# Half-size GpSimd subtractions in a Hymba decoder layer

## The chip, the cores and the metric

The kernel runs on one core of a Trainium2 chip. The metric is the device time of one execution in microseconds; less is better.

## The reference

One decoder layer over 512 tokens of width 1024, in float32. Cut to the parts that matter here:

```python
x = x + 0.5 * swiglu(rms_norm(x, ffn1_norm), ffn1_w_gate, ffn1_w_up, ffn1_w_down)   # D_FF = 2816
z = rms_norm(x, mix_norm) @ w_in            # 1024 -> 1280: pool group | q | k | v
merged = [rms_norm(causal_pool_mixer(u)), rms_norm(sliding_window_sink_attention(q, k, v))]
x = x + merged @ w_out
x = x + 0.5 * swiglu(rms_norm(x, ffn2_norm), ffn2_w_gate, ffn2_w_up, ffn2_w_down)
gate = sigmoid(rms_norm(x, ple_norm) @ w_ple_gate)
x = x + gate * (p @ w_ple_proj)
```

`swiglu(h, g, u, d)` is `(silu(h @ g) * (h @ u)) @ d`. All products are wanted at float32 precision.

## The kernel before, in words

Every product is made of three matmuls in the rounded type float32r: a matrix is split into a rounded part (hi) and the rest (lo), and hi x hi, lo x hi and hi x lo are summed in PSUM (`product`, L1584 to L1588). The kernel is written engine by engine, with counting semaphores between the engines; the order on each engine is the order in which the code stands.

**The weights.** They come in chunks of 128 partitions by 1024 columns, by DMAs on SyncE's queue, into a ring of four slots `raw`. ScalarE rounds a chunk into `w_hi` (`split`, L530). GpSimd subtracts: `w_lo = raw - w_hi` (`lo_of`, L403 to L406), and raises `w_ready`. TensorE waits for `w_ready` before it uses the chunk and raises `w_used` after it; SyncE waits for `w_ready` before it loads the slot again. GpSimd so makes 85 chunks' rests at L405. Its list mixes them with a few sums of the mixing stage (`win_sum`, `pool_sum`, `y_sum`).

**The gate and up projections of each FFN.** There are 22 column blocks f of 128. Four are plain. For the other 18, TensorE forms the two products with seven half-size products in place of eight, from sums of weight halves (Strassen's scheme in Winograd's form), in a loop over pairs of blocks. For each block VectorE makes the weight sums `sa` and `sb_f` (1024 columns each, `sums`, L1071 to L1078), ScalarE rounds them (L607, L616) and half of a gate chunk (L603), and GpSimd makes the rests in `fast_lo`: L415 (512 columns, the half gate chunk), L418 (1024, `sa`), L422 (1024, `sb_f`). The rest of the up chunk is made by VectorE itself (`u_rest`, L1083, 1024 columns). L422 waits for it:

```python
pool.wait_ge(sa_hi, m + 1)
pool.tensor_tensor(lo_at(sa_slot(c0, p)), sa[:], f32(hi_at(sa_slot(c0, p))),
                   ALU.subtract).then_inc(w_ready, 1)
pool.wait_ge(w_hi_done, f * 2 + c0 + 2)
pool.wait_ge(u_ready, m + 1)
```

On TensorE a block of the loop is seven parts of 12 matmuls (`pair`, L1654 to L1678). The first waits for `u_ready` (L1083), the second and third for `w_ready` (L418, L422), the last for `c_made`, the adds on VectorE at L1094, of which one stands behind L1083.

**The down projection of each FFN.** It runs in two halves of the output columns, 11 chunks each. The left operand is split anew for each chunk: ScalarE rounds (L631), VectorE makes the rest (`act_rest`, L1117, 1024 columns, both operands in SBUF). When the first half is complete, VectorE updates the residual: per block of 128 rows L1192 (PSUM times `rstd`) and L1194 (`x_t` plus `tmp`, both in SBUF, 512 columns). ScalarE then rounds the new `x_t` (L539) and squares it (L551), VectorE makes its rests (`h_rest`, L1022) and in the first FFN adds the squares (L1031). The roundings for the next chunks of the second half stand behind these in ScalarE's list, L1117 behind them in VectorE's.

**Other names.** In the fast loop's start VectorE makes sums of the left operand (L1126 to L1134) and their rests (L1059). L1431 is a rest of a sum in the mixing stage.

Of the kernel before, what the change touches and what calls it, by code (L numbers as in the profile page):

```python
# [7 lines left out]
ALU = mybir.AluOpType  # L8
# [10 lines left out]
def layer(nc, x, p, ffn1_norm, ffn1_w_gate, ffn1_w_up, ffn1_w_down, mix_norm, w_in, pool_w, pool_scale,  # L19
# [36 lines left out]
    WH = CHUNK // 2  # L56
# [11 lines left out]
    with es:  # L68
        def sb(name, shape, dt=F32, stack=es):
            return stack.enter_context(nc.sbuf_tensor(name, shape, dt))  # L70

        def sem(name):
            return es.enter_context(nc.semaphore(name))
# [17 lines left out]
        raw = sb("raw", [P, SLOTS, CHUNK])  # L91
        w_hi = sb("w_hi", [P, SLOTS, CHUNK], F32R)
        w_lo = sb("w_lo", [P, SLOTS, CHUNK], F32R)
# [7 lines left out]
        with ExitStack() as phase:  # L101
# [5 lines left out]
            sa = sb("sa", [P, CHUNK], stack=phase)  # L107
# [34 lines left out]
        sb_f = tmp[:, 2:4, :].rearrange("p a c -> p (a c)")  # L142
# [11 lines left out]
        def w_at(tile, extra, slot):  # L154
            return tile[:, slot, :] if slot < SLOTS else extra[:, slot - SLOTS, :]

        def hi_at(slot):
            return w_at(w_hi, wx_hi, slot)

        def lo_at(slot):  # L160
            return w_at(w_lo, wx_lo, slot)
# [4 lines left out]
        def sa_slot(c0, p):  # L166
            return (c0 + 2) % SLOTS if p else SLOTS

        def sb_slot(c0, p):
            return (c0 + 3) % SLOTS if p else SLOTS + 1  # L170

        def g_cols(p):
            return slice(p * WH, (p + 1) * WH)

        def raw_g(c0, p):
            return (c0 + 2 * p) % SLOTS
# [12 lines left out]
        w_hi_done, w_ready, w_used = sem("w_hi_done"), sem("w_ready"), sem("w_used")  # L189
# [51 lines left out]
        def f32(ap):  # L241

            return ap.bitcast(F32)
# [153 lines left out]
        def _(pool):  # L397
# [4 lines left out]

            def lo_of(slot, count):  # L403
                pool.wait_ge(w_hi_done, count)
                pool.tensor_tensor(w_lo[:, slot, :], raw[:, slot, :], f32(w_hi[:, slot, :]),  # L405
                                   ALU.subtract).then_inc(w_ready, 1)  # L406

            def fast_lo(n, c0):

                with pool.Fori(2, QUADS) as quad:  # L410
                    for p in range(2):
                        f = quad * 2 + p
                        m = f + n * FAST - PLAIN
                        pool.wait_ge(g_hi, m + 1)
                        pool.tensor_tensor(wx_lo[:, 2, g_cols(p)], raw[:, raw_g(c0, p), WH:],  # L415
                                           f32(wx_hi[:, 2, g_cols(p)]), ALU.subtract)
                        pool.wait_ge(sa_hi, m + 1)
                        pool.tensor_tensor(lo_at(sa_slot(c0, p)), sa[:], f32(hi_at(sa_slot(c0, p))),  # L418
                                           ALU.subtract).then_inc(w_ready, 1)
                        pool.wait_ge(w_hi_done, f * 2 + c0 + 2)  # L420
                        pool.wait_ge(u_ready, m + 1)
                        pool.tensor_tensor(lo_at(sb_slot(c0, p)), sb_f, f32(hi_at(sb_slot(c0, p))),  # L422
                                           ALU.subtract).then_inc(w_ready, 1)

            for slot in range(SLOTS):
                lo_of(slot, FFN1 + SLOTS + slot + 1)
            fast_lo(0, FFN1)
            with pool.Fori((FFN1 + GU) // SLOTS, (C_K + 2) // SLOTS) as quad:
                for slot in range(SLOTS):
                    lo_of(slot, quad * SLOTS + slot + 1)  # L430
# [40 lines left out]
            def y_sum(b):  # L471
# [6 lines left out]
                    .then_inc(y_summed, 1)  # L478

            lo_of(0, C_Q + 2)  # L480
            lo_of(1, C_Q + 3)
            lo_of(2, C_Q3 + 1)
# [26 lines left out]
            for c in range(C_WA + HALF - 1, FFN2 + 2 * SLOTS):  # L509
                lo_of(c % SLOTS, c + 1)  # L510
            fast_lo(1, FFN2)
            down = -(-(FFN2 + GU) // SLOTS)
            for c in range(FFN2 + GU, down * SLOTS):
# [1605 lines left out]
```

## Time and profile before

| what | value |
|---|---|
| time, median of 3 runs | 914.07 us (912.55 to 914.72) |
| the profiled execution's own time | 912.49 us |
| its span in the profile | 910.7 us |
| TensorE busy, matmuls | 893.5 us (98%) |
| VectorE / ScalarE / GpSimd busy | 541.8 / 496.5 / 475.3 us |
| GpSimd at L405 | 85 x 2587 ns = 219.2 us |
| GpSimd at L418 | 36, 96.3 us |
| GpSimd at L422 | 36 x 2402 ns = 86.4 us |
| GpSimd at L415 (512 columns) | 36 x 1312 ns = 47.2 us |

The span is what the profiler sees of the execution; 1.8 us of the execution's time lie outside it. Engines: PE is TensorE, DVE VectorE, ACT ScalarE, POOL GpSimd, SP SyncE. Busy time counts an operation from its start to its end in the record, so time in which an operation has started and waits inside the engine counts as busy.

### The profile page before, as it was taken

Reading aid. Unit: us, or ns where it says so; the run is one execution under the profiler, and the core shown is the slowest. Engines: PE = TensorE matmul, PEld = TensorE weight load, DVE = VectorE, ACT = ScalarE, POOL = GpSimd, SP = SyncE. Lnnn points to the kernel's source line nnn. Section 1 sums busy time; section 2 is a strip of 40 time slices with the busy share of each in tenths; the row PEclk is TensorE's granted clock in tenths of the full one; section 3 lists DMA queues with packets and bytes.
Section 4 is the critical chain, followed back from the end, with each engine's and each line's share of the span. In section 5 each row is a group of like instructions: output and inputs, shape, how many; then the busy total and the mean of one; then the engine's idle time right before and its main releaser. Section 6 shows DMA issues by size and latency. Waiting matters only on the chain.

```text
span 910.7 us, 15441 instructions
## 1 busy us (share of the span) xinstructions
PE 893.5 (98%) x5462; PEld 798.7 (88%) x5462; DVE 541.8 (59%) x819; ACT 496.5 (55%) x777; POOL 475.3 (52%) x228
## 2 busy tenths in 40 slices
PE   9989999999999999999999999999999999989998
PEld 7779999999988778887788879999999988878887
DVE  7586766676422733778958586667666522652552
ACT  5765666566433633668834756556655533433451
POOL 0446666666554364266665346666665564355430
PEclk9999999999999999999999999999999999999999
DMA  7523333333333244221324233333333253223311
GB/s 200 160 59 115 115 92 98 110 115 92 109 122 92 70 115 102 60 81 48 70 70 120 65 93 93 101 106 114 92 106 103 90 162 93 91 92 93 94 69 46
DMA packets 131049, 89.33 MB, mean 98 GB/s; under 512 B 11552, under 2 KB 116296, under 8 KB 131016
## 3 DMA queue, kind: packets, MB, share of 16 engines
q1 hardware_dynamic: 131000, 88.90, 32.9%
q8 instruction: 19, 0.31, 0.1%
q14 instruction: 14, 0.11, 0.0%
q10 hardware_dynamic: 16, 0.00, 0.0%
HBM read 86.80 MB, written 2.10 MB: 98 GB/s over the span
## 4 chain that ended last, share of the span: by engine, by line
PE 86%; DVE 7%; ACT 4%; issue 2%; DMA 0%; SPq 0%; DVEq 0%; ACTq 0%
PE bank L1586 28%; PE bank L1587 28%; PE bank L1588 28%; PE bank L1601 1%; DVE wx_lo L1117 1%; ACT act_f L579 1%; DVE x_t L1194 1%; ACT w_hi L530 1%; DVE tmp L1192 1%; PE bank L1857 1%; DVE w_lo L1083 1%; DVE act_f L1129 0%; ACT tmp L575 0%; DMA raw<-in_ffn_w_up 0%; DVE h_lo L1022 0%
## 5 line engine op out<-in xcount | busy, mean ns | idle before, releaser
L405 POOL TENSOR_TENSOR w_lo<-raw,w_hi 128x1024 fp32r<-128x1024 f32 x85 | 219.2, 2587 | 246.1 <-ACT w_hi L530 246.1
L1586 PE MATMUL bank<-h_hi,w_hi 128*128 128x256 f32 (+1 forms) x700 | 228.2, 326 | 3.9 <-DVE w_lo L1083 3.9
L1588 PE MATMUL bank<-h_hi,w_lo 128*128 128x256 f32 (+1 forms) x700 | 226.8, 324 | 0.0
L1587 PE MATMUL bank<-h_lo,w_hi 128*128 128x256 f32 (+1 forms) x700 | 226.8, 324 | 0.0
L1117 DVE TENSOR_TENSOR wx_lo<-act_f,wx_hi 128x1024 fp32r<-128x1024 f32 x44 | 65.7, 1497 | 145.7 <-ACT wx_hi L631 145.6
L1586 PEld LDWEIGHTS bank<-h_hi,w_hi 128*128 128x128 f32 x700 | 133.2, 190 | 16.0 <-DVE w_lo L1083 4.8
L1588 PEld LDWEIGHTS bank<-h_hi,w_lo 128*128 128x128 f32 x700 | 133.3, 190 | 10.7
L1586 PE MATMUL bank<-wx_hi,w_hi 128*128 128x512 f32 x352 | 137.9, 392 | 4.9 <-DVE wx_lo L1117 4.9
L1587 PEld LDWEIGHTS bank<-h_lo,w_hi 128*128 128x128 f32 x700 | 133.3, 190 | 10.0
L1587 PE MATMUL bank<-wx_lo,w_hi 128*128 128x512 f32 x352 | 137.7, 391 | 0.0
L1588 PE MATMUL bank<-wx_hi,w_lo 128*128 128x512 f32 x352 | 137.5, 391 | 0.0
L631 ACT ACTIVATE wx_hi<-act_f 128x1024 fp32r (+1 forms) x44 | 46.6, 1059 | 130.6 <-PE bank L1588 130.5
L530 ACT ACTIVATE w_hi<-raw 128x1024 fp32r<-128x1024 f32 x85 | 88.6, 1049 | 35.6 <-PE bank L1588 35.6
L415 POOL TENSOR_TENSOR wx_lo<-raw,wx_hi 128x512 fp32r<-128x512 f32 x36 | 47.2, 1312 | 94.9 <-ACT wx_hi L603 94.9
L1586 PEld LDWEIGHTS bank<-wx_hi,w_hi 128*128 128x128 f32 x352 | 66.5, 189 | 19.5 <-DVE wx_lo L1117 5.7
L1586 PE MATMUL bank<-xs_hi,wx_hi 128*128 128x256 f32 x288 | 82.3, 286 | 0.3 <-ACT sumsq L622 0.3
L1587 PE MATMUL bank<-xs_lo,wx_hi 128*128 128x256 f32 x288 | 82.1, 285 | 0.0
L1588 PE MATMUL bank<-xs_hi,wx_lo 128*128 128x256 f32 x288 | 82.0, 285 | 0.0
L1094 DVE TENSOR_TENSOR tmp<-bank,sumsq 128x256 f32<-128x256 f32 x72 | 30.6, 425 | 81.6 <-PE bank L1588 81.6
L1588 PEld LDWEIGHTS bank<-wx_hi,w_lo 128*128 128x128 f32 x352 | 66.5, 189 | 14.0
L1587 PEld LDWEIGHTS bank<-wx_lo,w_hi 128*128 128x128 f32 x352 | 66.4, 189 | 13.5
L575 ACT ACTIVATE tmp<-tmp 128x512 f32<-128x512 f32 x44 | 27.7, 630 | 91.6 <-DVE tmp L1100 85.1
(232 smaller groups left out, 1891.0 us busy)
## 6 DMA issues: line engine op xcount, KB each, us to landing
raw<-in_ffn_w_down SPq DMA_DIRECT2D x44, 512.0 KB, 3.7
raw<-in_ffn_w_gate SPq DMA_DIRECT2D x42, 512.0 KB, 3.8
raw<-in_ffn_w_up SPq DMA_DIRECT2D x42, 512.0 KB, 3.8
raw<-in_w_ple_gate SPq DMA_DIRECT2D x8, 512.0 KB, 3.7
raw<-in_w_in SPq DMA_DIRECT2D x6, 512.0 KB, 3.9
raw<-in_w_in SPq DMA_DIRECT2D x8, 256.0 KB, 3.5
raw<-in_w_out SPq DMA_DIRECT2D x4, 512.0 KB, 3.4
raw<-in_w_out SPq DMA_DIRECT2D x8, 256.0 KB, 4.1
```

The lines of the kernel that those rows point to most:

```text
L405: pool.tensor_tensor(w_lo[:, slot, :], raw[:, slot, :], f32(w_hi[:, slot, :]), ALU.subtract).then_inc(w_ready, 1)
L415: pool.tensor_tensor(wx_lo[:, 2, g_cols(p)], raw[:, raw_g(c0, p), WH:], f32(wx_hi[:, 2, g_cols(p)]), ALU.subtract)
L530: nc.scalar.activation(w_hi[:, slot, :], raw[:, slot, :], ACT.Copy).then_inc(w_hi_done, 1)
L575: nc.scalar.activation(a, a, ACT.Silu).then_inc(silu_done, 1)
L579: nc.scalar.activation(hf[d // HALF][:, d % HALF, :], x_t[:, d, :], ACT.Copy, scale=gain[:, 2 * n * KD + d:2 * n * KD + d + 1]).then_inc(h ...
L631: nc.scalar.activation(wx_hi[:, par, :].rearrange("p (a c) -> p a c", a=2), act_f[:, bass.ds((g - half) * 2, 2), :], ACT.Copy).then_inc(ac ...
L1083: nc.vector.tensor_tensor(lo_at(u_slot(c0, p)), raw[:, raw_u(c0, p), :], f32(hi_at(u_slot(c0, p))), ALU.subtract).then_inc(u_ready, 1)
L1094: nc.vector.tensor_tensor(dst, src[:, 0:TH], old, ALU.add).then_inc(c_made, 1)
L1117: nc.vector.tensor_tensor(wx_lo[:, par, :].rearrange("p (a c) -> p a c", a=2), act_f[:, bass.ds((g - half) * 2, 2), :], f32(wx_hi[:, par, ...
L1586: nc.tensor.matmul(dst, a_hi, b_hi, start=first, stop=False, skip_group_check=more)
L1587: nc.tensor.matmul(dst, a_hi, b_lo, start=False, stop=False, skip_group_check=more)
L1588: return nc.tensor.matmul(dst, a_lo, b_hi, start=False, stop=last, skip_group_check=more)
```

## The change

Each GpSimd subtraction of 1024 columns (`lo_of`, and the two of `fast_lo`) is written as two of 512 columns, one behind the other. The semaphore wait stands ahead of the first, the semaphore is raised by the second. `WH` is 512. Nothing else is changed.

```diff
             def lo_of(slot, count):
                 pool.wait_ge(w_hi_done, count)
-                pool.tensor_tensor(w_lo[:, slot, :], raw[:, slot, :], f32(w_hi[:, slot, :]),
+                pool.tensor_tensor(w_lo[:, slot, 0:WH], raw[:, slot, 0:WH], f32(w_hi[:, slot, 0:WH]), ALU.subtract)
+                pool.tensor_tensor(w_lo[:, slot, WH:], raw[:, slot, WH:], f32(w_hi[:, slot, WH:]),
                                    ALU.subtract).then_inc(w_ready, 1)
...
                         pool.wait_ge(sa_hi, m + 1)
-                        pool.tensor_tensor(lo_at(sa_slot(c0, p)), sa[:], f32(hi_at(sa_slot(c0, p))),
-                                           ALU.subtract).then_inc(w_ready, 1)
+                        lo, hi = lo_at(sa_slot(c0, p)), f32(hi_at(sa_slot(c0, p)))
+                        pool.tensor_tensor(lo[:, 0:WH], sa[:, 0:WH], hi[:, 0:WH], ALU.subtract)
+                        pool.tensor_tensor(lo[:, WH:], sa[:, WH:], hi[:, WH:], ALU.subtract).then_inc(w_ready, 1)
                         pool.wait_ge(w_hi_done, f * 2 + c0 + 2)
                         pool.wait_ge(u_ready, m + 1)
-                        pool.tensor_tensor(lo_at(sb_slot(c0, p)), sb_f, f32(hi_at(sb_slot(c0, p))),
-                                           ALU.subtract).then_inc(w_ready, 1)
+                        lo, hi = lo_at(sb_slot(c0, p)), f32(hi_at(sb_slot(c0, p)))
+                        pool.tensor_tensor(lo[:, 0:WH], sb_f[:, 0:WH], hi[:, 0:WH], ALU.subtract)
+                        pool.tensor_tensor(lo[:, WH:], sb_f[:, WH:], hi[:, WH:], ALU.subtract).then_inc(w_ready, 1)
```

The instructions of GpSimd before, from the chunks ahead of the fast loop (L405) to the first block of the loop's body, with the semaphores that they wait for:

```order
L405 TENSOR_TENSOR w_lo<-raw,w_hi 128x1024 [waits w_hi_done] x4
L410 UNCONDITIONAL_BRANCH
L410 ISA
L415 TENSOR_TENSOR wx_lo<-raw,wx_hi 128x512 [waits g_hi]
L418 TENSOR_TENSOR wx_lo<-sa,wx_hi 128x1024 [waits sa_hi]
L420 ISA
L422 TENSOR_TENSOR wx_lo<-tmp,wx_hi 128x1024 [waits u_ready,w_hi_done]
```

And the same stretch now, from the last of these chunks on:

```order
L405 TENSOR_TENSOR w_lo<-raw,w_hi 128x512 [waits w_hi_done]
L406 TENSOR_TENSOR w_lo<-raw,w_hi 128x512
L411 UNCONDITIONAL_BRANCH
L411 ISA
L416 TENSOR_TENSOR wx_lo<-raw,wx_hi 128x512 [waits g_hi]
L420 TENSOR_TENSOR wx_lo<-sa,wx_hi 128x512 [waits sa_hi]
L421 TENSOR_TENSOR wx_lo<-sa,wx_hi 128x512
L422 ISA
L425 TENSOR_TENSOR wx_lo<-tmp,wx_hi 128x512 [waits u_ready,w_hi_done]
L426 TENSOR_TENSOR wx_lo<-tmp,wx_hi 128x512
```

No instruction changes its place; each subtraction of 1024 columns is two rows, of which the second waits for no semaphore. The lists of the other engines are the same but for line numbers.

## Rows read from the trace of the kernel before

**Rows 1.** The page: busy time, share of the span and instructions by engine

```profile
PE 893.5 (98%) x5462; PEld 798.7 (88%) x5462; DVE 541.8 (59%) x819; ACT 496.5 (55%) x777; POOL 475.3 (52%) x228
```

**Rows 2.** Timeline, TensorE: start, us, operation, [idle before, who ended it]

```profile
57.75 0.39 PE L1586 MATMUL bank<-h_hi,w_hi 128*128 128x256 f32 x1 [2.96 <-DVE w_lo L1083]
68.42 0.39 PE L1586 MATMUL bank<-h_hi,wx_hi 128*128 128x256 f32 x1 [0.24 <-DVE tmp L1094]
...
319.95 0.50 PE L1586 MATMUL bank<-wx_hi,w_hi 128*128 128x512 f32 x1 [2.29 <-DVE wx_lo L1117]
...
540.45 0.39 PE L1586 MATMUL bank<-h_hi,w_hi 128*128 128x256 f32 x1 [0.96 <-DVE w_lo L1083]
...
802.96 0.64 PE L1586 MATMUL bank<-wx_hi,w_hi 128*128 128x512 f32 x1 [2.61 <-DVE wx_lo L1117]
```

**Rows 3.** Windows: stretch, us, busy (count) of PE, PEld, DVE, ACT, POOL, clock, DMA

```profile
803.00:807.00 4.00, 4.00 (x11) 3.17 (x12) 3.22 (x1) 0.00 (x0) 2.14 (x1) 0.57 0.50 154
320.00:324.00 4.00, 4.00 (x18) 3.27 (x19) 3.23 (x1) 0.00 (x0) 4.00 (x2) 1.00 0.57 166
```

**Rows 4.** Timeline, GpSimd and VectorE, start of the first fast loop

```profile
54.24 2.37 POOL L418 TENSOR_TENSOR wx_lo<-sa,wx_hi 128x1024 fp32r<-128x1024 f32 x1 [0.77 <-ACT wx_hi L607]
...
55.14 2.56 DVE L1083 TENSOR_TENSOR w_lo<-raw,w_hi 128x1024 fp32r<-128x1024 f32 x1 [0.75 <-ACT w_hi L612]
```

**Rows 5.** Timeline, VectorE and TensorE, inside the first fast loop

```profile
116.68 1.43 DVE L1083 TENSOR_TENSOR w_lo<-raw,w_hi 128x1024 fp32r<-128x1024 f32 x1
118.03 0.41 DVE L1094 TENSOR_TENSOR tmp<-bank,tmp 128x256 f32<-128x256 f32 x1
...
118.92 0.28 PE L1586 MATMUL bank<-h_hi,w_hi 128*128 128x256 f32 x1
```

**Rows 6.** Timeline, GpSimd and VectorE, residual update of the first FFN

```profile
303.47 2.48 POOL L405 TENSOR_TENSOR w_lo<-raw,w_hi 128x1024 fp32r<-128x1024 f32 x1 [2.96 <-ACT w_hi L530]
...
304.34 2.17 DVE L1194 TENSOR_TENSOR x_t<-x_t,tmp 128x512 f32<-128x512 f32 x1
306.55 0.69 DVE L1192 SCALAR_TENSOR_TENSOR tmp<-bank,rstd 128x512 f32<-128x512 f32 x1
307.27 0.69 DVE L1194 TENSOR_TENSOR x_t<-x_t,tmp 128x512 f32<-128x512 f32 x1
```

**Rows 7.** Timeline, GpSimd and VectorE, ahead of the gap at 319.95

```profile
315.80 3.02 POOL L405 TENSOR_TENSOR w_lo<-raw,w_hi 128x1024 fp32r<-128x1024 f32 x1 [9.85 <-ACT w_hi L530]
...
316.84 3.05 DVE L1117 TENSOR_TENSOR wx_lo<-act_f,wx_hi 128x1024 fp32r<-128x1024 f32 x1 [0.27 <-ACT wx_hi L631]
...
318.78 3.37 POOL L405 TENSOR_TENSOR w_lo<-raw,w_hi 128x1024 fp32r<-128x1024 f32 x1
```

**Rows 8.** Lines L405 and L415: duration ns min/median/max, first and last start

```profile
L405 POOL TENSOR_TENSOR w_lo<-raw,w_hi x85: 2391/2608/3387, 29.1 to 886.7; 128x1024 fp32r<-128x1024 f32 x85
...
L415 POOL TENSOR_TENSOR wx_lo<-raw,wx_hi x36: 1293/1300/1543, 52.2 to 706.5; 128x512 fp32r<-128x512 f32 x36
```

**Rows 9.** Timeline, ScalarE, VectorE and GpSimd, mixing stage

```profile
440.06 1.12 ACT L530 ACTIVATE w_hi<-raw 128x1024 fp32r<-128x1024 f32 x1
...
443.57 0.94 DVE L1431 TENSOR_TENSOR d_lo<-sumsq,d_hi 128x512 fp32r<-128x512 f32 x1
...
443.90 2.87 POOL L405 TENSOR_TENSOR w_lo<-raw,w_hi 128x1024 fp32r<-128x1024 f32 x1
```

**Rows 10.** Timeline, VectorE, second block of the second fast loop

```profile
548.67 2.05 DVE L1083 TENSOR_TENSOR w_lo<-raw,w_hi 128x1024 fp32r<-128x1024 f32 x1 [0.96 <-ACT w_hi L612]
```

**Rows 11.** Timeline, VectorE, ahead of the first fast loop

```profile
41.95 2.33 DVE L1129 TENSOR_TENSOR act_f<-act_f 128x1024 f32<-128x1024 f32 x1
```

**Rows 12.** Timeline, VectorE and GpSimd, ahead of the gap at 802.96

```profile
796.70 2.90 DVE L1022 SCALAR_TENSOR_TENSOR h_lo<-x_t,gain,h_hi 128x512 fp32r<-128x512 f32 x1
...
799.01 2.81 POOL L405 TENSOR_TENSOR w_lo<-raw,w_hi 128x1024 fp32r<-128x1024 f32 x1
...
799.52 3.38 DVE L1117 TENSOR_TENSOR wx_lo<-act_f,wx_hi 128x1024 fp32r<-128x1024 f32 x1
```

## The prediction

> **What bounds the kernel now.** I read the page first: TensorE is busy for 98% of the span [rows 1], so what can be won or lost lies in its few gaps or in a clock that falls. Then the timeline of TensorE, for its gaps. The reader is to see the five on which the sum rests: 2.96 us at 57.75 and 0.24 at 68.42 in the first FFN, 0.96 at 540.45 in the second, and 2.29 at 319.95 and 2.61 at 802.96, where each FFN's down projection passes from its first half of the output columns to its second [rows 2]. GpSimd ends none of them; VectorE does. The windows after two of them come next: after the gap of 2.61 us the granted clock averages 0.57 over 4 us (so most of it is at the lower level, 1.2 GHz), after the gap of 2.29 it stays at 1.00, 2.4 GHz [rows 3]. At 0.57, 4 us do the work of 2.28: 1.72 us lost.
>
> Then the timelines of VectorE and GpSimd beside each other, at the operations that end these gaps. GpSimd's subtract of 1024 columns runs from 54.24 to 56.61; VectorE's L1083, 1024 columns with both operands in SBUF, starts at 55.14 and ends at 57.70, 1.09 us after GpSimd [rows 4]. In the loop it takes 1.43 us [rows 5]. So it stood still until GpSimd was done and then ran. An operation of 512 columns does the same: L1194 starts at 304.34 behind a subtract that ends at 305.95 and ends at 306.51, 0.56 later; its unhindered neighbour L1194 takes 0.69 [rows 6]. L1192, which has one operand in PSUM, takes 0.69 as well [rows 6]. Call this a hold. GpSimd is held likewise: the subtract that starts at 318.78 ends at 322.15, 2.26 us after the L1117 that ended at 319.89 [rows 7].
>
> **What the change does to each operation.** 85 subtracts at L405 and 72 in the fast loop (36 at L418, 36 at L422) become 314 of 512 columns. The whole one takes 2.39 us at least; the 512-column form is there already, at L415, with 1.29 at least and 1.54 at most [rows 8]. One subtract starts some 0.04 us before the row of the one ahead ends (318.78 against 315.80 + 3.02 [rows 7]). So a pair takes 1.29 + 1.29 - 0.04 = 2.54, 0.14 more than a whole one of 2.40; bounds: 0 (no fixed part is added) and 2 x 1.54 - 2.40 = 0.68. I take 0.14, since an unhindered L415 is at its minimum. That is 157 x 0.14 = 22 us more of GpSimd time, on an engine that is 52% busy [rows 1], and off TensorE's path unless one result is late.
>
> The other side is the hold: it should end after 1.29 us, not 2.39, if the waiting VectorE operation gets its turn between the halves. What happens then, [rows 9] show. The subtract at 443.90 had its input from 441.18 on, since the last rounding at L530 ran from 440.06 to 441.18. VectorE's L1431 asked at 443.57, while the subtract before was running, and yet it went first: it ended at 444.51, and the subtract took 2.87 instead of 2.40. A waiting VectorE operation thus goes ahead of GpSimd's next one, even one that has long been ready. Held GpSimd work of 512 columns should end 2.26 - 1.10 = 1.16 after the VectorE operation that held it.
>
> **Term by term.**
> *Starts of the fast loop, 57.75 and 540.45.* The first half ends at 54.24 + 1.29 = 55.53, L1083 at 56.62, 1.08 us earlier. What follows on the way to the loop's steady state passes another L1083, 2.05 us long [rows 10], which asks so late that it meets the second half: 0.14 back. I allow 0.25 for L1059 in the same chain, which can now meet the halves of L422. Gain 0.7 each, 1.4 in all; bounds 0.3 and 1.08 each. The lower clock after 57.75 is not counted: the gap at 68.42 is ended by VectorE again, so that chain, not the matmuls, set the time there. L1129 before it, held for 2.33 us [rows 11], gives nothing: L1131 stands right behind it, has two SBUF operands too, and will meet the second half.
>
> *Down projection, 319.95.* L1194 ends at 303.47 + 1.29 + 0.56 = 305.32, 1.19 earlier. The second half starts then and ends at 306.48. The next L1194 would start at 306.08 and ends at 306.48 + 0.56 = 307.04 instead of 307.96: 0.92 stays of 1.19. From there VectorE and ScalarE pass this on to the subtract at 315.80 and L1117 at 316.84 [rows 7]. L1117 waits for all of a subtract that ended at 318.82; with halves it waits 1.10 less. Sum 0.92 + 1.10 = 2.02, less than the gap's 2.29. Gain 2.0; bounds 1.1 and 2.29.
>
> *Down projection, 802.96.* The same 0.92 at its L1194. Then L1022 at 796.70 took 2.90, held by a subtract, 1.10 less with halves. Then L1117 asked at 799.52 and ended at 802.90, behind the whole subtract that started at 799.01 [rows 12]. L1022 now ends at 799.60 - 0.92 - 1.10 = 797.58, the waiting half at 798.74, L1117 at 799.83: 3.07 earlier, more than the gap of 2.61, so TensorE goes through. With the gap goes the fall of the clock: 1.72. Gain 4.3; bounds 1.1 (half the gap, clock still falls) and 4.3.
>
> *Fast loop.* L1083 at 116.68 falls into the second half, which ends 0.14 later. The combining add behind it at 118.03 ends at 118.44, and the part of the matmuls that needs it starts at 118.92 [rows 5]: cover 0.48, of which 0.14 is used. Nothing.
>
> *Everything else* (w_lo in the mixing stage and at the end, loads that wait for it on SP's queue) is hidden behind TensorE: no gap over 0.2 us, there or anywhere, is ended by GpSimd. If a w_lo came late, TensorE would wait at its chunk.
>
> **The sum.** 1.4 + 2.0 + 4.3 = 7.7 us. The profiled execution took 912.49 (span 910.7), which gives 904.8; it lay 1.6 below the median of 914.07, from which I forecast 906.4.
>
> **Rivals.**
> *The halves keep the port between them.* They have no wait of their own between them, while the subtract of [rows 9] had one, though fulfilled. Then each hold lasts 0.14 longer: one each at the two loop starts, two at 319.95, three at 802.96, so 7 x 0.14 = 1.0 us slower, 915.1, within 0.2%. The Trainium skill has a rule for this, in "SBUF — State Buffer", section "Who interferes with whom": GpSimd and a VectorE operation with two SBUF inputs share a port pair, which the one that issues first keeps for its whole instruction. Whether the second half counts as issued behind its first, ahead of the VectorE operation, it does not tell; if it does, this rival is the rule's result. That a hold lasts as long as the instruction, [rows 4] show (1.09 us after its end). Against the rival: [rows 9]. Chance 0.13.
>
> *The gain is lost behind another wait.* L1117 is earlier, but ScalarE's roundings or a load ends the two gaps, and the clock still falls: some 1 us gained, 913, within 0.2%. For it: each gap is the end of a chain of some twenty operations. Against: the timeline shows VectorE as what ended each. Chance 0.05.
>
> *The loop becomes bound by GpSimd: slower.* If a half costs 1.54, the longest L415, a pair adds 0.68. In the loop that is over the cover of 0.48 by 0.20, in 36 rounds 7.2 us; and without a turn between the halves the seven holds grow by 0.68 each, 4.8. Together +12, 926. It decides from 0.48 us per pair, and even with turns from 0.70 it outweighs all gains (36 x 0.22 = 7.9). For it: L415 did take 1.54 once. Against: its median is 1.30 [rows 8]. Chance 0.05.
>
> **How the numbers follow.** Forecast 0.77, the rivals 0.13, 0.05 and 0.05. A measurement of this kernel can tell about 0.2%, 1.8 us, from no change. Forecast's own bounds: gains of 1.08 x 2 + 2.29 + 4.3 = 8.8 and 0.6 + 1.1 + 1.1 = 2.8, so 905.3 to 911.3; with 1.3 below for the spread of the runs, 904.0 to 911.3. That holds nearly all of 0.77, and with the edges of the second rival some 0.8. Faster by over 0.2%: 0.77. Within: 0.13 + 0.05 = 0.18. Slower: 0.05.
>
> **What would show it.** Right: 314 subtracts of 1.3 us in place of 157; L1083 near 55.1 takes some 1.5; L1117 before the second half of the down projection some 2.0 after 316; the gap at 802.96 gone and no window there below a clock of 0.9; L1083 in the loop at 1.57, without gaps of TensorE. Wrong: L1083 at 2.7 (no turn between halves), a gap per round of the loop, or a half that takes over 1.5.

## The result and the profile after

The changed kernel takes **905.0 us** (median of 4, 904.89 to 905.4), the kernel before 913.56 in the same comparison (912.55 to 914.72): ratio 0.9907, 95% interval 0.989 to 0.9924. Forecast were 906.4 in 904.0 to 911.3. The profiled execution took 905.06 with a span of 903.2, beside 912.49 and 910.7 before. Line numbers after L407 are higher by 3 in the changed kernel (L1083 is L1086, L1117 is L1120, L1194 is L1197).

The page's busy times, which answer to [rows 1]:

```profile
PE 891.0 (99%) x5462; PEld 796.6 (88%) x5462; DVE 530.4 (59%) x819; ACT 496.7 (55%) x777; POOL 509.0 (56%) x385
```

GpSimd has 157 instructions more and is busy 33.7 us longer; VectorE, with the same instructions, is busy 11.4 less.

TensorE's timeline after, all its gaps between 50 and 70 us, then the one at the start of the second fast loop (start, us, operation, [idle before, who ended it]):

```profile
56.87 0.39 PE L1589 MATMUL bank<-h_hi,w_hi 128*128 128x256 f32 x1 [1.88 <-DVE w_lo L1086]
60.62 0.38 PE L1589 MATMUL bank<-xs_hi,wx_hi 128*128 128x256 f32 x1 [0.62 <-POOL wx_lo L426]
64.43 0.38 PE L1589 MATMUL bank<-h_hi,wx_hi 128*128 128x256 f32 x1 [0.69 <-ACT sumsq L625]
67.94 0.39 PE L1589 MATMUL bank<-h_hi,wx_hi 128*128 128x256 f32 x1 [0.39 <-DVE tmp L1097]
...
540.83 0.38 PE L1589 MATMUL bank<-xs_hi,wx_hi 128*128 128x256 f32 x1 [0.62 <-POOL wx_lo L426]
```

The gap of 2.96 of [rows 2] is 1.88, 1.08 less. Two of 0.6 to 0.7 stand behind it that were not there, one of them ended by GpSimd, which ended none over 0.2 us before. By the gaps alone nothing was gained here: they sum to 3.20 us before and to 3.58 after. But before, TensorE ran the matmuls behind the first gap partly at 1.2 GHz (the windows stand with e1), and after at 2.4. What counts is when VectorE's chain lets the matmuls at 68.42 (67.94 after) start, and that is 0.48 us earlier, or 0.67 with the 0.19 by which this execution was late before the loop.

VectorE and GpSimd at the start of the first fast loop:

```profile
54.44 1.30 POOL L420 TENSOR_TENSOR wx_lo<-sa,wx_hi 128x512 fp32r<-128x512 f32 x1 [0.77 <-ACT wx_hi L610]
55.69 2.27 POOL L421 TENSOR_TENSOR wx_lo<-sa,wx_hi 128x512 fp32r<-128x512 f32 x1
...
55.33 1.48 DVE L1086 TENSOR_TENSOR w_lo<-raw,w_hi 128x1024 fp32r<-128x1024 f32 x1 [0.75 <-ACT w_hi L615]
```

L1086 asks while the first half runs and ends 1.07 us after that half. The second half ends 1.15 us after L1086. So VectorE gets its turn between the halves. Beside [rows 4], 2.56 became 1.48.

The same two engines at the residual update and the second half of the first FFN's down projection, which answer to [rows 6, 7], with TensorE's gap:

```profile
302.99 1.38 POOL L405 TENSOR_TENSOR w_lo<-raw,w_hi 128x512 fp32r<-128x512 f32 x1 [2.81 <-ACT w_hi L533]
304.33 1.75 POOL L406 TENSOR_TENSOR w_lo<-raw,w_hi 128x512 fp32r<-128x512 f32 x1
...
303.86 1.07 DVE L1197 TENSOR_TENSOR x_t<-x_t,tmp 128x512 f32<-128x512 f32 x1
...
305.69 0.95 DVE L1197 TENSOR_TENSOR x_t<-x_t,tmp 128x512 f32<-128x512 f32 x1
...
315.52 1.98 DVE L1120 TENSOR_TENSOR wx_lo<-act_f,wx_hi 128x1024 fp32r<-128x1024 f32 x1 [0.26 <-ACT wx_hi L634]
...
317.55 0.50 PE L1589 MATMUL bank<-wx_hi,w_hi 128*128 128x512 f32 x1 [0.36 <-DVE wx_lo L1120]
```

L1197 takes 1.07 where L1194 took 2.17, and L1120 1.98 where L1117 took 3.05. The gap of 2.29 is 0.36.

The window that answers to the first of [rows 3] (us, busy time and count of PE, PEld, DVE, ACT, POOL, granted clock, DMA share, GB/s); the same matmuls start 5.7 us earlier now, at 797.3. Then VectorE ahead of it, for [rows 12]:

```profile
797.30:801.30 4.00, 4.00 (x19) 3.33 (x18) 1.65 (x1) 2.01 (x2) 3.70 (x3) 1.00 0.51 171
```

```profile
794.63 2.31 DVE L1120 TENSOR_TENSOR wx_lo<-act_f,wx_hi 128x1024 fp32r<-128x1024 f32 x1
798.79 1.65 DVE L1120 TENSOR_TENSOR wx_lo<-act_f,wx_hi 128x1024 fp32r<-128x1024 f32 x1 [1.85 <-ACT wx_hi L634]
```

There is no gap, and the granted clock is 1.00 (2.4 GHz) where its mean was 0.57.

Where the 7.45 us between the two profiles went, from the starts of the same matmuls in both, read at the last matmul of each place (minus is earlier):

| place | forecast | measured |
|---|---|---|
| the kernel's first 50 us | 0 | +0.19 |
| start of the first fast loop | -0.7 | -0.67 |
| down projection, 319.95 | -2.0 | -1.92 |
| mixing stage | 0 | +0.15 |
| start of the second fast loop | -0.7 | -0.68 |
| down projection, 802.96 | -4.3 | -4.52 |

### The profile page after: what moved, and what is told of

Read it like the earlier page. It is cut to its first block, busy times and chain, and to the rows that moved or that the text cites. A ratio compares the mean times of both kernels' runs of the same rounds, so it can differ in the third digit from the quotient of the medians.

```text
span 903.2 us, 15598 instructions
## 1 busy us (share of the span) xinstructions
PE 891.0 (99%) x5462; PEld 796.6 (88%) x5462; DVE 530.4 (59%) x819; ACT 496.7 (55%) x777; POOL 509.0 (56%) x385
## 4 chain that ended last, share of the span: by engine, by line
PE 88%; DVE 5%; ACT 4%; issue 2%; POOL 1%; DMA 0%; SPq 0%; DVEq 0%; POOLq 0%; ACTq 0%
PE bank L1589 29%; PE bank L1590 28%; PE bank L1591 28%; PE bank L1604 1%; ACT act_f L582 1%; ACT w_hi L533 1%; PE bank L1860 1%; DVE act_f L1134 0%; DVE wx_lo L1120 0%; DMA raw<-in_ffn_w_up 0%; ACT tmp L578 0%; DVE x_t L1197 0%; DVE sumsq L1034 0%; DVE tmp L1195 0%; POOL wx_lo L425 0%
## 5 line engine op out<-in xcount | busy, mean ns | idle before, releaser
L405 POOL TENSOR_TENSOR w_lo<-raw,w_hi 128x512 fp32r<-128x512 f32 x85 | 122.1, 1437 | 221.4 <-ACT w_hi L533 221.4
L1120 DVE TENSOR_TENSOR wx_lo<-act_f,wx_hi 128x1024 fp32r<-128x1024 f32 x44 | 58.2, 1322 | 149.6 <-ACT wx_hi L634 149.6
L406 POOL TENSOR_TENSOR w_lo<-raw,w_hi 128x512 fp32r<-128x512 f32 x85 | 121.9, 1434 | 0.0
```

The costliest lines, as they stand in the source:

```text
L405: pool.tensor_tensor(w_lo[:, slot, 0:WH], raw[:, slot, 0:WH], f32(w_hi[:, slot, 0:WH]), ALU.subtract)
L406: pool.tensor_tensor(w_lo[:, slot, WH:], raw[:, slot, WH:], f32(w_hi[:, slot, WH:]), ALU.subtract).then_inc(w_ready, 1)
L1120: nc.vector.tensor_tensor(wx_lo[:, par, :].rearrange("p (a c) -> p a c", a=2), act_f[:, bass.ds((g - half) * 2, 2), :], f32(wx_hi[:, par, ...
```

## The experiments

Theory A: a VectorE operation with two SBUF operands, which a running GpSimd subtract holds up, gets its turn at the boundary of two GpSimd instructions, so halving them shortens its wait. The rivals were that something else of the change gives the time, that the halves keep the port, and that the wait itself decides, not the size.

### e1: only L405 halved

```diff
-                pool.tensor_tensor(w_lo[:, slot, :], raw[:, slot, :], f32(w_hi[:, slot, :]),
+                pool.tensor_tensor(w_lo[:, slot, 0:WH], raw[:, slot, 0:WH], f32(w_hi[:, slot, 0:WH]), ALU.subtract)
+                pool.tensor_tensor(w_lo[:, slot, WH:], raw[:, slot, WH:], f32(w_hi[:, slot, WH:]),
                                    ALU.subtract).then_inc(w_ready, 1)
```

> Only the 85 subtractions at L405 are halved; sa and sb_f stay whole. Theory (VectorE gets its turn between the halves, each place adds up by itself): the two residual updates gain as in the changed kernel, 1.9 at the first and 4.5 at the second (its gap and the fall of the clock), 0.15 is lost in the mixing stage, the two loop starts gain nothing: 6.3 us less than before, some 907.3. L1083 at 55.1 still takes 2.5 us. Rival (the gain comes from GpSimd being finer everywhere, loops included): clearly less than 5 us gained.

Measured: 906.45 (906.31 to 907.09), ratio 0.9922 (0.9909 to 0.9935). In its profile the matmuls gain 1.97 at 319.95 and 4.52 at 802.96 and lose 0.15 in the mixing stage, which is within 0.05 of the changed kernel's own figures. At the first loop's start it loses 0.56 to the kernel before. The windows there show why, first of e1, then of the kernel before:

```profile
58.00:62.00 4.00, 3.87 (x18) 3.87 (x19) 2.06 (x4) 2.41 (x4) 2.39 (x1) 0.50 0.48 141
62.00:66.00 4.00, 4.00 (x28) 4.00 (x28) 3.02 (x5) 2.06 (x5) 2.63 (x2) 0.74 0.43 121
```

```profile
58.00:62.00 4.00, 4.00 (x24) 0.63 0.54 153
62.00:66.00 4.00, 4.00 (x33) 0.94 0.35 105
```

Behind the same gap of 2.96 (2.95 here) TensorE ran longer at 1.2 GHz. This varies from execution to execution. The changed kernel's profile, with 1.88 in its place, shows no lower clock there; that of e2, with the same 1.88, does (0.62 from 57 to 61 us).

### e2: only the fast loop's subtracts halved

```diff
-                        pool.tensor_tensor(lo_at(sa_slot(c0, p)), sa[:], f32(hi_at(sa_slot(c0, p))),
-                                           ALU.subtract).then_inc(w_ready, 1)
+                        lo, hi = lo_at(sa_slot(c0, p)), f32(hi_at(sa_slot(c0, p)))
+                        pool.tensor_tensor(lo[:, 0:WH], sa[:, 0:WH], hi[:, 0:WH], ALU.subtract)
+                        pool.tensor_tensor(lo[:, WH:], sa[:, WH:], hi[:, WH:], ALU.subtract).then_inc(w_ready, 1)
...
```

> Only sa and sb_f (72 subtractions) are halved; L405 stays whole. Theory: 0.67 + 0.68 gained at the two loop starts, nothing in the loops, the gaps of 2.3 and 2.6 us at the residual updates stay and with the second the fall of the clock: 1.35 less than before, 912.2. If the 4 us behind the second gap stay at the full clock here, the fall of the clock hangs on something else than that gap.

Measured: 911.62 (909.62 to 913.25, 12 runs), ratio 0.9976 (0.9965 to 0.9986). The loop starts gain 0.71 and 0.69. Added by place, e1's 6.34 (without the clock at its first loop start) and these 1.40 are 7.74, and the change itself has 7.64 (7.45 and the 0.19 of its first 50 us): the places are independent of each other. The two gaps of the down projections, which the edit does not touch, are still there, and show that my reading of [rows 3] was chance:

```profile
319.67 0.50 PE L1588 MATMUL bank<-wx_hi,w_hi 128*128 128x512 f32 x1 [2.29 <-DVE wx_lo L1119]
...
803.60 0.50 PE L1588 MATMUL bank<-wx_hi,w_hi 128*128 128x512 f32 x1 [2.63 <-DVE wx_lo L1119]
```

```profile
320.00:324.00 4.00, 4.00 (x12) 3.15 (x11) 2.93 (x1) 0.00 (x0) 4.00 (x2) 0.59 0.53 172
...
804.00:808.00 4.00, 4.00 (x19) 3.31 (x18) 2.88 (x1) 0.00 (x0) 1.79 (x1) 1.00 0.58 173
```

Here the clock falls behind the gap of 2.29 (1.6 us lost to the kernel before) and not behind the one of 2.63 (1.6 won). Whether the clock falls behind such a gap changes between executions; behind the 2.29 of e4 below it does not fall either.

### e4: one single subtract halved, that of chunk 145

```diff
+                if split:
+                    pool.tensor_tensor(w_lo[:, slot, 0:WH], raw[:, slot, 0:WH], f32(w_hi[:, slot, 0:WH]), ALU.subtract)
+                    pool.tensor_tensor(w_lo[:, slot, WH:], raw[:, slot, WH:], f32(w_hi[:, slot, WH:]),
+                                       ALU.subtract).then_inc(w_ready, 1)
+                    return
...
+                lo_of(c % SLOTS, c + 1, c == 145)
```

> Of all 157, only one subtraction is halved, that of chunk 145, which starts at 799.01 and holds L1117 ahead of the gap at 802.96. Theory: L1117 ends 1.1 us earlier, the gap shrinks from 2.6 to 1.5, and, as after the gap of 2.3 in the first FFN, the clock does not fall: 1.1 + 1.7 = 2.8 less than before, 910.7. Rival (the clock falls there after any gap): 1.1 less, 912.4, and a window of 4 us behind the gap at 0.57.

Measured: 911.46 (909.95 to 912.2), ratio 0.9976 (0.9967 to 0.9986). In the profile 2.67 us are gained at 802.96: 1.07 because the gap is 1.55 in place of 2.61, and 1.60 because the clock stays up:

```profile
803.00:807.00 4.00, 4.00 (x19) 3.31 (x18) 1.61 (x1) 0.04 (x1) 3.87 (x2) 1.00 0.44 143
```

Only the 1.07 is surely the split's: e2 kept the clock up behind the whole gap of 2.63. By the interval of the ratio this one split is worth 1.3 to 3.0 us of the change's 8.6. The loop start lost 0.6, as in e1.

### e3: quarters everywhere

```diff
+                for i in range(4):
+                    cols = slice(i * CHUNK // 4, (i + 1) * CHUNK // 4)
+                    ins = pool.tensor_tensor(w_lo[:, slot, cols], raw[:, slot, cols], f32(w_hi[:, slot, cols]), ALU.subtract)
+                ins.then_inc(w_ready, 1)
```

(and so for both subtracts of the fast loop)

> Every subtraction as four of 256 columns. Theory: what counts is how long after VectorE's request the running piece ends. L1083 asks 0.9 us after the start of L418; halves let it in at 1.29, quarters (0.74 alone, 0.70 from one to the next) at 1.44, so quarters are no better there, and four cost 0.4 more than a whole one, which the results for the second and third part of the loop's first block and the mixing stage pay. 0.5 to 2.5 us slower than halves: 905.5 to 907.5. Rival (finer is better, the hold shrinks with the piece): faster than halves, under 904.5. Second rival (the loop's cover of 0.48 is used up): a gap in each round, 36 x 0.1 or more, over 908.

Measured: 913.59 (910.59 to 915.57, 11 runs), ratio 0.9993 (0.9981 to 1.0004): missed, no better than the kernel before. The trace has what no theory had. L1125 (L1117 before) at 248.75, the GpSimd rows around it, and TensorE behind it:

```profile
248.75 7.09 DVE L1125 TENSOR_TENSOR wx_lo<-act_f,wx_hi 128x1024 fp32r<-128x1024 f32 x1 [5.05 <-ACT wx_hi L639]
```

```profile
243.59 11.17 POOL L407 TENSOR_TENSOR w_lo<-raw,w_hi 128x256 fp32r<-128x256 f32 x16 [2.92 <-ACT w_hi L538]
```

```profile
255.89 0.50 PE L1594 MATMUL bank<-wx_hi,w_hi 128*128 128x512 f32 x1 [2.84 <-DVE wx_lo L1125]
...
257.84 0.63 PE L1595 MATMUL bank<-wx_lo,w_hi 128*128 128x512 f32 x1
```

Behind the fast loop four chunks are rounded at once, so GpSimd has 16 quarters ready, one starting every 0.70 us (11.17 / 16). VectorE asked at 248.75 and stood for 6.0 us, past eight boundaries, until all 16 were done at 254.76; then it ran, so that its row is 7.09 long. TensorE waits 2.84 and falls to 1.2 GHz (0.63 a matmul in place of 0.39), which costs 4.8 together. At the same place of the second FFN VectorE stands as long again and TensorE waits 2.84 again, but the clock stays up (3.1 lost). Elsewhere quarters do as theory A says: the second halves of the down projections gain 2.20 and 4.52. A price that the expectation had is there too: at the second loop's start GpSimd's own result is late, in this profile and in all the others of quarters:

```profile
547.80 0.38 PE L1594 MATMUL bank<-xs_hi,wx_hi 128*128 128x256 f32 x1 [2.01 <-POOL wx_lo L430]
```

### e5: quarters, each at L405 with a fulfilled wait of its own

```diff
                 for i in range(4):
+                    if i:
+                        pool.wait_ge(w_hi_done, count)
```

(the quarters of the fast loop as in e3, without it)

> Quarters at L405 again, but each of the four waits for w_hi_done, which is already fulfilled for the second to fourth. The quarters without it had two holds of 7.1 us, at 248.75 and 733.22, where a backlog of nine ready quarters ran through without a turn for VectorE. Theory A (pieces without a wait of their own are taken up so early, with a growing overlap of their rows, that the port never gets free): the waits bring the turn back, both holds fall under 2 us, the two gaps of 2.8 us and one fall of the clock go, 6 to 7 us faster than quarters, 907 to 908. Theory B (length of the backlog or of the piece alone decides): the holds of 7.1 us stay, 912 to 914.

Measured: 910.64 (906.37 to 915.15, 12 runs), ratio 0.9979 (0.9961 to 0.9998), in three groups, near 906.5, 910 and 914. The median is in neither theory's range. The profiled one, 906.62, has no long wait. The runs e10 to e12 below take this up.

### e6: subtracts whole, but two of them placed behind the VectorE work

```diff
+                if c == (58, 143)[n]:
+                    pool.wait_ge(act_ready, n * 2 * DH + DH + 4)
```

> No subtraction is halved. GpSimd takes up chunks 58 and 143 only when VectorE's L1117 ahead of the two gaps is done. Theory (the gaps were made by holds, nothing else): L1194, L1022 and L1117 on the way take their free 0.69, 0.75 and 1.23 us, both gaps close, 2.3 and 4.5 us gained, 6.8 less than before, 907 to 907.5, more than halving L405 alone at these two places. Rival (the halves gain by something other than shorter holds, or the later w_lo makes TensorE wait): less than 4 us gained.

Measured: 907.87 (median of five, 907.33 to 909.24; a sixth execution took 1781.89, as one of the kernel before in the same comparison took 4931.17, which nothing here explains), ratio 0.9939 (0.9925 to 0.9953). The collisions are gone without any split:

```profile
304.92 0.69 DVE L1207 TENSOR_TENSOR x_t<-x_t,tmp 128x512 f32<-128x512 f32 x1
...
315.98 1.23 DVE L1130 TENSOR_TENSOR wx_lo<-act_f,wx_hi 128x1024 fp32r<-128x1024 f32 x1 [0.27 <-ACT wx_hi L644]
```

```profile
317.28 8.05 POOL L405 TENSOR_TENSOR w_lo<-raw,w_hi 128x1024 fp32r<-128x1024 f32 x3 [16.19 <-DVE wx_lo L1130]
```

```profile
319.78 0.49 PE L1599 MATMUL bank<-wx_hi,w_hi 128*128 128x512 f32 x1 [1.54 <-POOL w_lo L405]
```

So it is the collision that cost the time, not GpSimd's work. At 802.96 this gains 4.45, as the halves do. At 319.95 it gains only 0.78, where the expectation had the gap close: GpSimd starts so late that its own w_lo ends TensorE's gap.

### e7: the change, and one rounding on ScalarE earlier

```diff
                 split(c0 + SLOTS + 2)
+                split(c0 + SLOTS + 3)
                 for d in range(HALF, KD):
                     h_gained(n, d)
-                split(c0 + SLOTS + 3)
```

> The changed kernel, with ScalarE's rounding of the last plain chunk one step earlier (before the second four gained rows), so that GpSimd's halves of it lie before L1131 asks. L1131 (held 1.1 us for the second half, as forecast) is then free, L1129 held by 0.6. Theory: the chains to both loop starts are 0.6 us shorter: 1.2 less than the changed kernel, 903.8. Rival (TensorE is held by GpSimd's rest of sb there, 0.62 us, or by ScalarE): within 0.4 of 905.0.

Measured: **903.81** (903.54 to 904.03, 4 runs), ratio 0.9891 (0.9877 to 0.9906) to the kernel before, the fastest of all. The gap in the first loop's start is 0.62 less than after the change:

```profile
56.56 0.38 PE L1589 MATMUL bank<-h_hi,w_hi 128*128 128x256 f32 x1 [1.26 <-DVE w_lo L1086]
```

The second loop's start gains 0.67 over the change. The reason is the one expected, one more collision. VectorE's sums of the left operand ahead of the loop, first after the change, then in e7:

```profile
42.13 1.22 DVE L1132 TENSOR_TENSOR act_f<-act_f 128x1024 f32<-128x1024 f32 x1
43.28 2.32 DVE L1134 SCALAR_TENSOR_TENSOR act_f<-act_f 128x1024 f32<-128x1024 f32 x1
```

```profile
42.46 1.69 DVE L1132 TENSOR_TENSOR act_f<-act_f 128x1024 f32<-128x1024 f32 x1
44.07 1.21 DVE L1134 SCALAR_TENSOR_TENSOR act_f<-act_f 128x1024 f32<-128x1024 f32 x1
```

After the change L1134 is held by the second half, 1.10 over its free 1.22. In e7 both halves lie earlier, since ScalarE's rounding that feeds them does; L1134 is free and L1132 is held for 0.47. The difference, 0.63, is the gain.

### e8: e7 with the two waits of e6

> The changed kernel with both: the earlier rounding and GpSimd's wait for L1117 at chunks 58 and 143. Adds to the previous one what is left of the first residual update's gap, 0.4 us: 903.4. If the two places were not independent of each other, it differs from the previous one by more than 1 us.

Measured: 905.29 (905.01 to 905.88), ratio 0.9909 (0.9896 to 0.9922): slower than e7, where 903.4 was expected. At the second half of the first down projection w_lo is late even in halves, some 1.3 us lost to e7:

```profile
318.75 0.49 PE L1602 MATMUL bank<-wx_hi,w_hi 128*128 128x512 f32 x1 [1.69 <-POOL w_lo L406]
```

### e9: quarters, but halves where many are ready at once

```diff
+            for c in range(FFN1 + GU, 13 * SLOTS):
+                lo_of(c % SLOTS, c + 1, 2)
...
             for c in range(FFN2 + GU, down * SLOTS):
-                lo_of(c % SLOTS, c + 1)
+                lo_of(c % SLOTS, c + 1, 2)
```

> Every subtract in four pieces, except the chunks behind each fast loop (44 to 51 and 129 to 135), which are in halves as in the change: there the kernel of quarters had 16 ready pieces in a row and VectorE's L1125 stood for 7.1 us, twice. Theory A (a long row of ready 256-column pieces is what VectorE gets no turn in): L1125 at 248 and 733 takes under 2.4 us, all runs within 905.5 to 908.5, median 907. Rival B (short pieces give no turn anywhere, by chance of the moment): other holds over 3 us appear in this profile, or the runs still scatter from 906 to 915, median 909 to 913.

Measured: 906.57 (906.06 to 907.5), ratio 0.9923 (0.991 to 0.9937), as theory A has it. The scatter is gone with the long rows of small pieces: the five runs lie within 1.4 us, and one long wait is worth 3 (below). The same VectorE instruction, and GpSimd's eight halves in a row:

```profile
247.80 2.20 DVE L1127 TENSOR_TENSOR wx_lo<-act_f,wx_hi 128x1024 fp32r<-128x1024 f32 x1 [5.05 <-ACT wx_hi L641]
```

```profile
242.64 11.01 POOL L407 TENSOR_TENSOR w_lo<-raw,w_hi 128x512 fp32r<-128x512 f32 x8 [3.21 <-ACT w_hi L540]
```

It waits for the half that runs and goes ahead of the next. The kernel is still 1.6 us slower than the change, as the theory of e3 had it for quarters (0.5 to 2.5).

### e10, e11, e12: further profiles of the two kernels of quarters

> The kernel of quarters once more, for a second profile of it. Theory A: both holds of 7.1 us are there again, at the same two instructions, and the time is 913 to 914; at 910.6 one of them would be missing. Rival B: they are at other places.

Measured: 914.16, with one long wait, the second; at 250.98 L1125 took 1.54:

```profile
250.98 1.54 DVE L1125 TENSOR_TENSOR wx_lo<-act_f,wx_hi 128x1024 fp32r<-128x1024 f32 x1 [5.05 <-ACT wx_hi L639]
```

The time was near the expected one, for another reason: its matmuls were already 2.2 us later than in e12 at 21 us, in the start that no edit touches, and the second wait cost 4.8 with the fall of the clock behind it.

> The kernel of quarters with a fulfilled wait ahead of each piece, for a second profile. Theory A (its runs at 910 and 914 have one and two holds of 7.1 us at L1127, those at 906.5 none): the time names the number of holds, 906.5, 910 or 914 for none, one or two. Rival (the wait gives VectorE its turn every time and the scatter is something else, such as the clock): no hold over 3 us, whatever the time.

> As the run before it, a third profile: theory A: 906.5, 910 or 914 for none, one or two holds of 7.1 us at L1127. Rival: no hold over 3 us, whatever the time.

Measured: 910.17 and 907.12, the same program twice. VectorE at the place in question and GpSimd's rows around it, first in e11, then in e12:

```profile
729.82 7.08 DVE L1127 TENSOR_TENSOR wx_lo<-act_f,wx_hi 128x1024 fp32r<-128x1024 f32 x1 [5.05 <-ACT wx_hi L641]
```

```profile
728.83 2.84 POOL L409 TENSOR_TENSOR w_lo<-raw,w_hi 128x256 fp32r<-128x256 f32 x4
```

```profile
729.89 1.54 DVE L1127 TENSOR_TENSOR wx_lo<-act_f,wx_hi 128x1024 fp32r<-128x1024 f32 x1 [5.05 <-ACT wx_hi L641]
```

```profile
728.89 3.13 POOL L409 TENSOR_TENSOR w_lo<-raw,w_hi 128x256 fp32r<-128x256 f32 x3
```

In e12 a piece is held while VectorE goes ahead; in e11 the pieces pass one after the other, the first four in 2.84 us, and VectorE's row is 7.08 long. All matmuls behind are 3.05 us later in e11, and so differ the runs. So a long wait is worth 3 us, or 4.8 where the clock falls behind it, and a fulfilled wait on a semaphore between the pieces does not prevent it. In the five profiles of kernels with 16 quarters in a row there were ten occasions, and VectorE missed its turn at four (both in e3, one each in e10 and e11). Why at these four stays open: between e11 and e12 VectorE asked at the same point of the piece to some hundredths of a us (0.29 and 0.30 after its start).

## Why the prediction was right

**Starts of the fast loop, 0.7 each.** Measured 0.67 and 0.68, by the steps of the working. The first gap shrank by 1.08. Both operations that were named as giving back did so, L1059 (L1062 now), which meets L426, and the next block's L1083 (L1086 now), which meets the second half of `sa`:

```profile
60.93 1.22 DVE L1059 TENSOR_TENSOR h_lo<-act_f,h_hi 128x1024 fp32r<-128x1024 f32 x1 [1.17 <-ACT h_hi L586]
...
65.97 2.06 DVE L1083 TENSOR_TENSOR w_lo<-raw,w_hi 128x1024 fp32r<-128x1024 f32 x1
```

```profile
60.05 1.49 DVE L1062 TENSOR_TENSOR h_lo<-act_f,h_hi 128x1024 fp32r<-128x1024 f32 x1 [1.18 <-ACT h_hi L589]
...
65.36 2.19 DVE L1086 TENSOR_TENSOR w_lo<-raw,w_hi 128x1024 fp32r<-128x1024 f32 x1 [0.96 <-ACT w_hi L615]
```

They give back 0.27 (0.25 allowed) and 0.13 (0.14 worked out), and 1.08 - 0.40 is 0.68. The gaps of 0.62 and 0.69 that GpSimd's L426 and ScalarE's L625 now end were not named, but they lie off this chain: ScalarE's rows between L1062 and L1086 keep the spacing that they had before. Before, the matmuls there ran partly at the lower clock, and that filled the time in which they stand idle now. L1129 ahead of the loop gave nothing, as said, since the next operation met the second half; e7 shows that this second collision was worth another 0.6 at each start.

**Down projection at 319.95, 2.0.** Measured 1.92. Its parts are in the rows. After takes 0.48 off every time by here (0.67 less 0.19), so the first L1197 ends 306.51 - 0.48 - 304.93 = 1.10 earlier, where 1.19 was worked out, and the second 307.96 - 0.48 - 306.64 = 0.84, where 0.92 was. L1120 waits 1.07 less, where 1.10 was. (The L1192 of [rows 6], at 306.55, says nothing of PSUM operands, since no subtract runs beside it. The one before it does: it starts at 303.62, inside the subtract of 303.47, and takes 0.68.) e6 shows the cause by another way: without the collision the same operations take 0.69 and 1.23.

**Down projection at 802.96, 4.3.** Measured 4.52: 2.78 by the gap and 1.74 by the fall of the clock. L1117 was worked out to end at 799.83; less the 2.93 by which the changed kernel is ahead there this is 796.90, and it ended at 796.94. e4 gets 1.07 of the gap from one subtract. The mechanism held, but the sentence that this gap makes the clock fall and that of 319.95 does not was a reading of one execution: e2 shows it the other way round. So it was partly luck that the sum came out so near: it counts one fall behind the two gaps, which both this profile and e2's have, but e4's has none behind the same 2.29. What the removed gaps gave back themselves is 1.92 and 2.78 us, and a fall is 1.6 to 1.7 more in those executions where it followed.

**Split at no cost to TensorE.** A pair has two rows of 1.28 to 1.30 that overlap by 0.04, as in the working (the unhindered halves at 444.62 and 445.87 are 1.25 apart, 2.54 for the pair). The 22 us of more GpSimd time came out as 33.7, since halves are now themselves held more often, which was not counted: L420's wx_lo averages 1.66. In the loop L1086 takes 1.56 to 1.58, where 1.57 was named, and no gap came. "Everything else hidden" was wrong by 0.15 in the mixing stage. It is the operation of [rows 9], L1431 (L1434 now), which asks while a second half runs and so waits for the 0.14 that a pair takes more:

```profile
440.40 1.31 POOL L406 TENSOR_TENSOR w_lo<-raw,w_hi 128x512 fp32r<-128x512 f32 x1
...
441.18 1.07 DVE L1434 TENSOR_TENSOR d_lo<-sumsq,d_hi 128x512 fp32r<-128x512 f32 x1
```

It took 0.94 before; the VectorE operation behind it and the matmul at 443.06 are later by as much. e1 has the same 0.15. The working had this term, 0.14 for a collision with a second half, and did not look for it here.

**From the profile to the median.** This is the step that failed, though inside the range. I carried the 1.6 us between the profiled execution and the median over to the changed kernel. But those 1.6 are for the most part falls of the clock behind gaps, which differ from execution to execution (0.6 more behind 57.75 in e1 and e4, 1.6 more behind one down projection and 1.6 less behind the other in e2). The mean granted clock of each execution bears this out: of the 27 of the kernel before that were taken beside e1 to e4, the 14 at 0.994 took 914.25 to 915.11 but for one (913.14), and the 13 at 0.995 to 0.998 took 912.44 to 913.13 but for two (914.58 and 914.60). The profiled one had 0.996. The first 30 us, in which the profiles differ by up to 1.1 us (e10 apart), can add to it. The change removes most of these gaps: the profile of after, 905.06, lies at its median, 905.0, and its four runs span 0.5 us where those of before span 2.2. So the medians differ by 8.6 and the profiles by 7.4.

**The rivals.** That the halves keep the port between them is out for this kernel: in the profile of after some 120 VectorE operations met a subtract; one went ahead of the half that had just started, all others ran when that half ended, and none passed a boundary. The gain was not lost behind another wait either: of the gaps of the down projections 0.36 us is left, and the chain behind took 0.4 back at a loop start, as forecast. The Trainium skill's rule, in "SBUF — State Buffer", section "Who interferes with whom", that the one which issues first keeps the shared port for its whole instruction, agrees with these rows (L1086 ends 1.07 after the half). What it leaves open, the turn between back-to-back instructions, came out in two ways here: it was VectorE's with halves, and not always with quarters. My argument from [rows 9], that a fulfilled wait between the two might matter, did not decide: halves without a wait hand over, quarters with one sometimes do not (e11). The slower case asked for 1.54 us for a half; the unhindered ones take 1.3, and no gap per round appeared.

## What to carry to other kernels

Where GpSimd and a VectorE operation with two operands in SBUF meet ahead of TensorE, the wait is what is left of the running GpSimd instruction, so find the few instructions that collide on the path: one of the 157 splits gave 1.07 us of gap, and the clock's 1.60 with it where a fall would have followed. A collision moves when what stands ahead of it does, as e7 shows, so look for the next one after each change. Halving cost 0.14 us a pair on an engine that had the room. Smaller is not better: in quarters the same split, repeated in a long ready row, sometimes shut VectorE out for 6 us and gave nearly the whole gain back. Delaying the GpSimd work works as well, but only as far as its own result is not due. Before carrying a median's offset over, ask what makes it; if it is the clock behind the gaps that the change removes, it goes with them.

## What was not expected of the hardware

- VectorE missed its turn at eight boundaries one after the other in rows of 16 GpSimd subtracts of 256 columns (0.70 us from one start to the next), at 4 of 10 occasions, and never in rows of 512 columns (1.25 us apart; some 120 meetings in the profile of after and eight halves in a row in e9, none past a boundary).
- A GpSimd subtract costs near 0.15 us and 1.1 us per 512 columns, an estimate from the spacing in rows without a wait: 0.70, 1.25 and 2.35 us from start to start for 256, 512 and 1024 columns.
- The gaps of 2.29 and of 2.61 to 2.63 us on TensorE are each followed by 1.2 GHz in one execution and not in another of the same stretch, which alone moves the time by 1.6 us. What decides it, no run here shows.
